# State-space scan of a hybrid decoder step: RMSNorm gains as a column table on ScalarE, sums made in y, two planes of decays instead of three

## The chip, the cores and the metric

The kernel runs on 1 core of a Trainium2 chip. The metric is the device time of one launch in microseconds (us), the median of several runs. A profiled execution of the same program gives a span (first to last instruction) and, slightly longer, a time of its own.

## The reference, cut to what matters

One layer of a decoder: a Mamba-2 branch (chunked scan), a latent attention branch, a gated merge, and a mixture of experts. Only the end of the scan branch is touched by the change. For each group `g` of 4 and each tile of tokens it computes

```
a_cs  = cumsum(dt * a)                                   # per head, within a chunk of 128 tokens
decay = exp(where(causal, a_cs[l] - a_cs[s], -inf))      # one 128x128 plane per head
y     = ((cm @ bm.T) * decay * dt) @ x  +  (cm @ h_prev) * exp(a_cs)
y     = y + ssd_d * x
y     = y * silu(z)
y     = y * rsqrt(mean(y * y, -1) + RMS_EPS) * ssd_norm_g   # RMSNorm over the 512 channels of a group
y_a   = y @ w_branch_a                                   # needs y turned: channels on partitions
```

There are 512 prompt tokens (4 tiles of 128 rows) and 64 sample tokens (8 sequences of 8, one tile of 64 rows, which start from stored states), 4 groups of 8 heads with 64 channels each.

## The kernel before

The program is a row of stages with a barrier between them: latents, two attentions, a first merge, the convolution, the scan (`stage_ssd`), a second merge, the choice of experts, the experts. Each stage is written once for each engine, and the order in an engine's code is the order of execution; engines meet only at semaphores.

The scan stage runs over 20 units. Unit `k` is group `g = k // 5` and tile `i = k % 5`; tile 4 is the sample tile. What follows uses these names.

**Decays.** `dec` holds planes of 8 heads x 128 x 128. SP (the queue of DMA requests) fills plane `k % 3` with a broadcast of rows of the running sums (`decays`, L1422 to L1426, 512 KB). VectorE subtracts each row's own sum in place (L1837, eight TENSOR_SCALAR), ScalarE takes the exponent in place (`decay`, L1683), VectorE multiplies by C.B (`weigh`, L1814), TensorE reads the plane (`outputs`, L1570). A plane is free when `y_ready` counts its unit.

**SP.** At the start it requests planes 0, 1 and 2, the gate weights of group 1, the 2 MB of stored states of group 0 and the gains of groups 0 and 1. Then for each `k` it waits for `y_ready` k + 1 and requests plane k + 3. After the sample tile of a group (`i == 4`) it goes through `new_states` (L1428 to L1434): it waits until VectorE has renewed the states, requests 2 MB of stores, waits until these stores have landed, and requests 2 MB of stored states of the next group (`old_states`, L1420). At the first tile of a group it also requests 2 MB of gate weights (L1415), waits for `normed` and requests gains (L1437).

**TensorE** in round `k`: `inputs(k)` (x, B and C.B, L1527 to L1534), `gate(k-1)` (z, L1558, the longest part), `turn(k-2)` (y turned into bank 0, L1638; waits for `normed`), `outputs(k-1)` (L1570 to L1576; gives `y_ready`, and `st_ready`).

**VectorE** in round `k`: copies and the subtraction of unit `k` (L1825 to L1837), then y of unit `k-1`: `off` = bank 5 times exp(a_cs) (L1857), y = off + xd (L1863), y += bank 4 (L1865), y *= silu(z) (L1868), the state (L1872, L1874), `weigh(k)` (L1814), and the norm: y times 1/rms times the gains `gn`, 128 x 512, broadcast to all partitions by DMA (L1889).

**ScalarE** in round `k`: `copy_x(k)` (L1678), `gate_out(k-1)` (L1696), `turned_y(k-2)` (L1702: one copy of 128x512 from bank 0 to `yT`), `decay(k)` (L1683), `root(k-1)` (L1724, L1726). Around a sample tile it also copies turned states (L1709, L1717).

**GpSimd** scales x by dt, by the end weights and by D (L1483).

Of the kernel before, what the change touches and what calls it, by code (L numbers as in the profile page):

```python
# [12 lines left out]
ALU = mybir.AluOpType  # L13
ACT = mybir.ActivationFunctionType
AX = mybir.AxisListType.X

P = 128
# [5 lines left out]
NT = 5  # L23
# [9 lines left out]
G, HG, PD, NST = 4, 8, 64, 128  # L33
SH = G * HG
GW = HG * PD
# [1317 lines left out]
def stage_ssd(nc, io, sb):  # L1353

    with ExitStack() as ctx:
        sem = ctx.enter_context(signals(nc, "ssd"))
        buf = lambda n, s: ctx.enter_context(nc.sbuf_tensor(n, s, F32))
# [3 lines left out]
        wz = (sb.wz0, buf("wz1", [P, KD, GW]))  # L1361
        m_raw, _ = merge_room(sb)
        dt_b, a_b, d_b = buf("dt_b", [P, SH]), buf("a_b", [P, SH]), buf("d_b", [P, SH])
        gn = buf("gn", [P, 2, GW])
        t1, t23 = buf("t1", [P, NT, SH]), buf("t23", [P, 2 * NT * SH])
        t2, t3 = (t23[:, NT * SH * j:NT * SH * (j + 1)].rearrange("p (i h) -> p i h", i=NT) for j in range(2))
        dta, acs, aend, e_acs, w_end, e_end = (buf(n, [P, NT, SH]) for n in ("dta", "acs", "aend", "e_acs", "w_end", "e_end"))
# [2 lines left out]
        xs_t = buf("xs_t", [P, 2, GW])  # L1370
        b_t = buf("b_t", [P, 2, NST])
        cb = buf("cb", [P, P])
        dec = buf("dec", [P, 3, HG, P])
        xdt, xend, xd = buf("xdt", [P, 2, GW]), buf("xend", [P, 2, GW]), buf("xd", [P, 2, GW])
        y = buf("y", [P, 2, GW])
        off = buf("off", [P, GW])
        zs = buf("zs", [P, GW])
        junk = zs
        ssq = buf("ssq6", [P, 2])
# [6 lines left out]
        banks = ctx.enter_context(nc.psum_tensor("banks6", [P, 8, 512], F32))  # L1386
        N = G * NT
# [5 lines left out]
        xs_ready, xs_out, cb_ready, cb_out, seg_out, dec_out, w_out = (sem(n) for n in (  # L1393
            "xs_ready", "xs_out", "cb_ready", "cb_out", "seg_out", "dec_out", "w_out"))
        scaled, of_seq, z_ready, z_out, y_ready, y_step, gated, squared, rooted, inverse, normed = (sem(n) for n in (
            "x_scaled", "of_seq", "z_ready", "z_out", "y_ready", "y_step", "gated", "squared6", "rooted6", "inverse", "normed6"))
# [2 lines left out]
            "hT_ready", "hT_out", "hT_out2", "off_part", "fin_ready", "fin_out", "hs_ready", "hs_out"))  # L1399
        e_out, y_sum, mean_ready = sem("e_out"), sem("y_sum"), sem("mean_ready")  # L1400
        rows_out, rows_in, aged = sem("rows_out"), sem("rows_in"), sem("aged")
        gn_in = [sem("gn_in0"), sem("gn_in1")]
        dec_in = [sem(f"dec_in{j}") for j in range(3)]
        heads = lambda t, n: t.rearrange("p (h d) -> p h d", h=HG)
        z_view = io.w_in.rearrange("(k p) n -> p k n", p=P)
        tri = lambda i, n: K[0:n, K_TRI:K_TRI + n] if i < 4 else K[0:n, K_BTRI:K_BTRI + n]
# [1 line left out]
        with nc.Block() as block:  # L1408
            @block.sync
            def _(sp):  # L1410
                for t, src in ((dt_b, io.dt_bias), (a_b, io.a_log), (d_b, io.d_skip)):
                    sp.dma_start(t[:], src.broadcast_to((P, SH))).then_inc(vec_in, 16)

                def z_weights(g):
                    sp.dma_start(wz[g % 2][:], z_view[:, :, C_Z + g * GW:C_Z + (g + 1) * GW]).then_inc(wz_in[g % 2], 16)  # L1415

                def old_states(g):
                    for q in range(4):
                        at = g * GW + q * P
                        sp.dma_start(h0[:, q], io.ssm[:, at:at + P, :].rearrange("b p n -> p b n")).then_inc(h_in, 16)  # L1420

                def decays(k):  # L1422
                    g, i = unit(k)
                    n = ROWS[i]
                    at = i * SH + g * HG
                    sp.dma_start(dec[0:n, k % 3, :, 0:n], io.acs_rows[at:at + HG, 0:n].unsqueeze(0).broadcast_to((n, HG, n))).then_inc(dec_in[k % 3], 16)  # L1426

                def new_states(g):  # L1428
                    sp.wait_ge(fin_out, g + 1)
                    sp.dma_start(io.o_ssmp[g * GW:(g + 1) * GW, :].rearrange("(q p) n -> p q n", p=P), st_out).then_inc(p_out, 16)  # L1430
                    sp.wait_ge(hs_out, 8 * (g + 1))
                    for q in range(4):
                        at = g * GW + q * P
                        sp.dma_start(io.o_ssms[:, at:at + P, :].rearrange("b p n -> p b n"), h0[:, q]).then_inc(h_out, 16)  # L1434

                def norm_gains(g):
                    sp.dma_start(gn[:, g % 2], io.gn[:, g * GW:(g + 1) * GW].broadcast_to((P, GW))).then_inc(gn_in[g % 2], 16)  # L1437

                z_weights(0)
                sp.wait_ge(rows_out, 1)  # L1440
                sp.dma_start(io.acs_rows[0:4 * SH, :], acsT[:, 0, :]).then_inc(rows_in, 16)
                sp.dma_start(io.acs_rows[4 * SH:5 * SH, 0:NS], acsT[0:SH, 1, 0:NS]).then_inc(rows_in, 16)
                sp.wait_ge(rows_in, 32)
                for k in range(3):
                    decays(k)
                z_weights(1)
                old_states(0)
                for g in range(2):
                    norm_gains(g)
                for k in range(N):  # L1450
                    g, i = unit(k)
                    sp.wait_ge(y_ready, k + 1)
                    if k + 3 < N:
                        decays(k + 3)
                    if i == NT - 1:
                        new_states(g)
                        if g + 1 < G:
                            sp.wait_ge(h_out, 64 * (g + 1))
                            old_states(g + 1)
                    if i == 0 and 1 <= g < G - 1:  # L1460
                        sp.wait_ge(z_ready, NT * g)
                        z_weights(g + 1)
                        sp.wait_ge(normed, NT * g)
                        norm_gains(g + 1)
                    if i == 0 and g == G - 1:
                        sp.wait_ge(z_ready, NT * g)
                        for u in range(2):
                            sp.dma_start(m_raw[:, u], merge_view(io, u)).then_inc(sb.raw_in[u], 16)
# [34 lines left out]
            def _(pe):  # L1503
# [57 lines left out]
                def outputs(k):  # L1561
# [5 lines left out]
                    if k >= 1:  # L1567
                        pe.wait_ge(y_step, 2 * k)
                    for h in range(HG):
                        pe.matmul(banks[0:n, 4, h * PD:(h + 1) * PD], dec[0:n, k % 3, h, 0:n], xdt[0:n, k % 2, h * PD:(h + 1) * PD], start=True, stop=True)  # L1570
                    if i < NT - 1:
                        pe.wait_ge(st_new, NT * g + i + 1)
                        if g >= 1 and i == 0:
# [84 lines left out]
            def _(act):  # L1658
# [21 lines left out]
                def decay(k):  # L1680
                    n = ROWS[unit(k)[1]]
                    act.wait_ge(seg_out, k + 1)
                    act.activation(dec[0:n, k % 3, :, 0:n], dec[0:n, k % 3, :, 0:n], ACT.Exp).then_inc(dec_out, 1)  # L1683

                def gate_out(j):
                    i = unit(j)[1]
# [11 lines left out]
                def turned_y(j):  # L1698
                    g, i = unit(j)
                    n = ROWS[i]  # L1700
                    act.wait_ge(yt_ready, j + 1)
                    act.activation(sb.yT[:, 4 * g:4 * g + 4, P * i:P * i + n], banks[:, 0, 0:4 * n].rearrange("p (q n) -> p q n", q=4),  # L1702
                                   ACT.Copy).then_inc(yt_out, 1)

                def last_state(g):
                    act.wait_ge(fin_ready, g + 1)
# [48 lines left out]
            def _(dve):  # L1755
# [52 lines left out]

                def weigh(k):
                    n = ROWS[unit(k)[1]]  # L1810
                    seg = dec[0:n, k % 3, :, 0:n]
                    dve.wait_ge(dec_out, k + 1)
                    dve.wait_ge(cb_out, k + 1)
                    dve.tensor_tensor(seg, seg, cb[0:n, 0:n].unsqueeze(1).broadcast_to((n, HG, n)), ALU.mult).then_inc(w_out, 1)  # L1814

                for k in range(N + 1):
                    if k < N:
# [12 lines left out]
                            dve.sem_inc(cb_out, 1)  # L1830
                        else:
                            ins.then_inc(cb_out, 1)
                        seg = dec[0:n, k % 3, :, 0:n]
                        dve.wait_ge(dec_in[k % 3], 16 * (k // 3 + 1))
                        for h in range(HG):
                            own = acs[0:n, i, g * HG + h:g * HG + h + 1]
                            ins = dve.tensor_scalar(seg[:, h, :], seg[:, h, :], own, 0.0, ALU.subtract, ALU.min)  # L1837
# [3 lines left out]
                    if k >= 1:  # L1841
# [4 lines left out]
                        if i == NT - 1:  # L1846
                            for m in range(4):
# [6 lines left out]
                                if m == 1 and k < N:  # L1854
                                    weigh(k)
                        dve.wait_ge(y_ready, j + 1)
                        dve.tensor_tensor(heads(off[0:n], n), heads(banks[0:n, 5, :], n), e_acs[0:n, i, hs].unsqueeze(2).broadcast_to((n, HG, PD)),  # L1857
                                          ALU.mult).then_inc(y_step, 1)
                        dve.wait_ge(y_step, 2 * j + 1)
                        if j >= 2:  # L1860
                            dve.wait_ge(yt_ready, j - 1)
                        dve.wait_ge(scaled, j + 1)
                        dve.tensor_tensor(y[0:n, j % 2, :], off[0:n], xd[0:n, j % 2, :], ALU.add).then_inc(y_sum, 1)  # L1863
                        dve.wait_ge(y_sum, j + 1)
                        dve.tensor_tensor(y[0:n, j % 2, :], y[0:n, j % 2, :], banks[0:n, 4, :], ALU.add).then_inc(y_step, 1)  # L1865
                        dve.wait_ge(y_step, 2 * j + 2)
# [16 lines left out]
                        if i < NT - 1:  # L1883
# [1 line left out]
                        dve.wait_ge(rooted, j + 1)  # L1885
                        dve.reciprocal(ssq[0:n, 1:2], ssq[0:n, 1:2]).then_inc(inverse, 1)
                        dve.wait_ge(inverse, j + 1)
                        dve.wait_ge(gn_in[g % 2], 16 * (g // 2 + 1))
                        dve.scalar_tensor_tensor(out=y[0:n, j % 2, :], in0=y[0:n, j % 2, :], scalar=ssq[0:n, 1:2],  # L1889
                                                 in1=gn[0:n, g % 2], op0=ALU.mult, op1=ALU.mult).then_inc(normed, 1)  # L1890
                        if i == NT - 1:
                            renew(j, 2)
                            renew(j, 3)
# [1028 lines left out]
```

## Time and profile before

| | us |
|---|---|
| median of 3 runs | 2441.16 |
| the runs | 2435.20 to 2441.32 |
| profiled execution, its own time | 2435.43 |
| its span | 2433.7 |
| mean granted TensorE clock in it | 0.965 |

The stage of the scan lies at about 669 to 975 us of the span; its units run from about 690 to 970. All times in rows are counted from the start of the span. A duration of matmuls on TensorE can overlap the next by a little. SPq rows are requests: the duration is how long SP was busy giving the request out, and the time to landing is told apart, in an answer for that line.

### The profile page before, as it was taken

How to read it: one execution, taken by the hardware profiler on the slowest of the kernel's cores; microseconds unless marked ns; L12 is line 12 of the kernel's file. 1: busy time of each engine (PE TensorE's matmuls, PEld its weight loads, DVE VectorE, ACT ScalarE, POOL GpSimd, SP SyncE). 2: the span in 40 equal slices, each digit the busy share in tenths (PEclk: the TensorE clock that was granted, in tenths of full speed). 3: DMA queues.
4: the chain of work that ended last, by engine and by line, in shares of the span. 5: the costliest groups of instructions: out<-in, count | busy, mean ns of one | idle time of the engine just before them, and what ended most of it. 6: DMA issues, size and time to landing. Idle time of an engine off the chain costs nothing. (4 is left out here: it accounts for less than half of the span.)

```text
span 2433.7 us, 38463 instructions
## 1 busy us (share of the span) xinstructions
PE 2295.1 (94%) x14433; PEld 1856.1 (76%) x14433; DVE 1841.7 (76%) x2278; ACT 1323.0 (54%) x1416; POOL 476.2 (20%) x414
## 2 busy tenths in 40 slices
PE   8898999989879998998979999999999999999997
PEld 4486778989845554997767888888888888888885
DVE  2577774167657777344578999999999999999997
ACT  1352224133245555422337777777777777777774
POOL 0003320000024443000143222122122212211223
PEclk9998998989989998998979999999999999999999
DMA  5106753232153332323559999999999999999995
GB/s 173 67 1 232 284 188 87 53 94 86 41 160 120 108 123 80 106 82 141 183 161 361 394 394 396 391 382 382 396 384 379 384 392 383 381 395 382 380 381 191
DMA packets 248676, 589.96 MB, mean 242 GB/s; under 512 B 28945, under 2 KB 120338, under 8 KB 244082
## 3 DMA queue, kind: packets, MB, share of 16 engines
q1 hardware_dynamic: 230874, 510.39, 57.3%
q0 software_dynamic: 17680, 77.88, 10.1%
q8 instruction: 84, 1.38, 0.2%
q14 instruction: 38, 0.31, 0.0%
HBM read 552.43 MB, written 35.80 MB: 242 GB/s over the span
## 5 line engine op out<-in xcount | busy, mean ns | idle before, releaser
L2694 DVE TENSOR_TENSOR w_lo<-w_raw,w_hi 128x2048 fp32r<-128x2048 f32 x291 | 658.6, 2288 | 52.7 <-ACT w_hi L2639 50.5
L2639 ACT ACTIVATE w_hi<-w_raw 128x2048 fp32r<-128x2048 f32 x288 | 550.2, 1916 | 116.5 <-PE banks L2549 89.6
L2549 PE MATMUL banks<-w_hi,x_hi 128*128 128x512 f32 x1024 | 319.5, 393 | 3.9 <-DVEq L2739 3.3
L2549 PE MATMUL banks<-w_lo,x_hi 128*128 128x512 f32 x1024 | 316.5, 390 | 0.0
L2549 PE MATMUL banks<-w_hi,x_lo 128*128 128x512 f32 x1024 | 315.9, 390 | 0.0
L2694 DVE TENSOR_TENSOR w_lo<-mergedT,w_hi 128x2048 fp32r<-128x2048 f32 x96 | 220.1, 2292 | 31.7 <-ACT w_hi L2639 31.1
L2549 PEld LDWEIGHTS banks<-w_hi,x_lo 128*128 128x128 f32 x1024 | 192.5, 188 | 40.9
L2549 PEld LDWEIGHTS banks<-w_lo,x_hi 128*128 128x128 f32 x1024 | 192.5, 188 | 40.8
L2549 PEld LDWEIGHTS banks<-w_hi,x_hi 128*128 128x128 f32 x1024 | 190.1, 188 | 42.3 <-DVEq L2739 3.7
L2497 POOL DMA_INDIRECT y_sum<-xT,to_row x31 | 51.0, 1645 | 823.5 <-ACT xT L2676 780.7
L2639 ACT ACTIVATE w_hi<-mergedT 128x2048 fp32r<-128x2048 f32 x96 | 183.8, 1915 | 33.7 <-PE banks L2549 30.7
L2549 PE MATMUL banks<-w_hi,h_hi 128*128 128x512 f32 x512 | 161.7, 397 | 1.2 <-DVE h_lo L2698 0.8
L2549 PE MATMUL banks<-w_lo,h_hi 128*128 128x512 f32 x512 | 158.8, 392 | 0.0
L2549 PE MATMUL banks<-w_hi,h_lo 128*128 128x512 f32 x512 | 158.2, 390 | 0.0
L1558 PE MATMUL banks<-wz,xT 128*128 128x512 f32 x256 | 113.6, 596 | 0.0
L2549 PEld LDWEIGHTS banks<-w_hi,h_lo 128*128 128x128 f32 x512 | 96.4, 188 | 20.9
L2549 PEld LDWEIGHTS banks<-w_lo,h_hi 128*128 128x128 f32 x512 | 96.4, 188 | 20.7
L2549 PEld LDWEIGHTS banks<-w_hi,h_hi 128*128 128x128 f32 x512 | 93.9, 189 | 19.7 <-issue 1.2
L1153 DVE TENSOR_TENSOR w_mlo_a<-wz,w_mhi_a 128x1024 fp32r<-128x1024 f32 x24 | 29.4, 1226 | 82.4 <-ACT w_mhi_a L1127 82.4
L1117 PE MATMUL banks_a<-part_hi_a,w_mhi_a 128*128 128x288 f32 x384 | 83.4, 299 | 8.8 <-DVE w_mlo_a L1153 8.8
L1558 PEld LDWEIGHTS banks<-wz,xT 128*128 128x128 f32 x256 | 47.6, 191 | 56.1 <-issue 56.1
L1483 POOL TENSOR_TENSOR xdt<-xs_t,dt 128x512 f32<-128x512 f32 (+1 forms) x20 | 27.2, 1360 | 318.7 <-ACT xs_t L1678 297.7
(511 smaller groups left out, 4591.2 us busy)
## 6 DMA issues: line engine op xcount, KB each, us to landing
w_raw<-in_exp_w_gu SPq DMA_DIRECT2D x196, 1024.0 KB, 10.3
w_raw<-in_exp_w_down SPq DMA_DIRECT2D x96, 1024.0 KB, 7.8
mergedT<-in_exp_w_gu SPq DMA_DIRECT2D x64, 1024.0 KB, 10.2
mergedT<-in_exp_w_down SPq DMA_DIRECT2D x32, 1024.0 KB, 10.0
w_x<-in_w_in SPq DMA_DIRECT2D x11, 1024.0 KB, 5.2
wz<-in_w_in SPq DMA_DIRECT2D x4, 2048.0 KB, 11.2
dec<-acs_rows SPq DMA_DIRECT2D x16, 512.0 KB, 4.2
states<-in_state_ssm SPq DMA_DIRECT2D x16, 512.0 KB, 6.8
```

Of the source, the lines that this page charges most:

```text
L1117: mm = pe.matmul(bank_of(u)[:, piece], wp[:, u % NW, k, :], part[:, piece * H2:(piece + 1) * H2], start=(k == 0 and wp is w_hi and n == 0) ...
L1153: dve.tensor_tensor(w_lo[:, u % NW], w_raw[:, u % NR], w_hi[:, u % NW].bitcast(F32), ALU.subtract).then_inc(w_low, 1)
L1483: ins = pool.tensor_tensor(heads(o[0:n, k % 2], n), x, f[:, g * HG:(g + 1) * HG].unsqueeze(2).broadcast_to((n, HG, PD)), ALU.mult)
L1558: mm = pe.matmul(banks[0:n, 7, :], sb.xT[:, q, P * i:P * i + n], wz[g % 2][:, q, :], start=(q == 0), stop=(q == KD - 1))
L2497: pool.indirect_dma_start(out=io.y_sum, out_offset=bass.IndirectOffsetOnAxis(ap=to_row[:, par, :].bitcast(U32), axis=0), in_=y_out, in_off ...
L2549: mm = pe.matmul(banks[:, bank + c, :], x[:, k, :], part[:, s % NHI, j, c * 512:(c + 1) * 512], start=start, stop=last)
L2639: act.activation(w_hi[:, s % NHI], raw(s, par), ACT.Copy).then_inc(hi_ready, 1)
L2694: dve.tensor_tensor(w_lo[:, s % NHI], raw(s, par), w_hi[:, s % NHI].bitcast(F32), ALU.subtract).then_inc(lo_ready, 1)
```

## The change

Four things, all in `stage_ssd`:

- The gains are read once as `gnT`, 128 x 16: column `t` holds the gains of channels 128t to 128t + 127. VectorE's last step is a TENSOR_SCALAR by 1/rms alone, and `turned_y` on ScalarE makes four copies of 128 columns with a column of `gnT` as scale, where it made one of 512. The first of them waits for `gnT`.
- `off` is gone: the product is written to `y`, with the wait for `yt_ready` moved ahead of it, and xd is added in place.
- `dec` has two planes, `k % 2`; SP requests 0 and 1 at the start, and plane k + 2 after `y_ready` k + 1.
- SP's waits for `normed` and its requests of gains (four of 256 KB) are gone; one request of 2048 elements of 4 bytes takes their place.

```diff
-        gn = buf("gn", [P, 2, GW])
+        gnT = buf("gnT", [P, G * 4])
-        dec = buf("dec", [P, 3, HG, P])
+        dec = buf("dec", [P, 2, HG, P])
-        off = buf("off", [P, GW])
...
-                for k in range(3):
+                for k in range(2):
                     decays(k)
                 z_weights(1)
                 old_states(0)
-                for g in range(2):
-                    norm_gains(g)
+                sp.dma_start(gnT[:], io.gn.rearrange("o (t p) -> p (o t)", p=P), allow_slow_non_contiguous=True).then_inc(gn_in, 16)
                 for k in range(N):
                     g, i = unit(k)
                     sp.wait_ge(y_ready, k + 1)
-                    if k + 3 < N:
-                        decays(k + 3)
+                    if k + 2 < N:
+                        decays(k + 2)
...
                     if i == 0 and 1 <= g < G - 1:
                         sp.wait_ge(z_ready, NT * g)
                         z_weights(g + 1)
-                        sp.wait_ge(normed, NT * g)
-                        norm_gains(g + 1)
...
                     act.wait_ge(yt_ready, j + 1)
-                    act.activation(sb.yT[:, 4 * g:4 * g + 4, P * i:P * i + n], banks[:, 0, 0:4 * n].rearrange("p (q n) -> p q n", q=4),
-                                   ACT.Copy).then_inc(yt_out, 1)
+                    if j == 0:
+                        act.wait_ge(gn_in, 16)
+                    for q in range(4):
+                        t = 4 * g + q
+                        ins = act.activation(sb.yT[:, t, P * i:P * i + n], banks[:, 0, q * n:(q + 1) * n], ACT.Copy, scale=gnT[:, t:t + 1])
+                    ins.then_inc(yt_out, 1)
...
-                        dve.tensor_tensor(heads(off[0:n], n), heads(banks[0:n, 5, :], n), e_acs[0:n, i, hs].unsqueeze(2).broadcast_to((n, HG, PD)),
+                        if j >= 2:
+                            dve.wait_ge(yt_ready, j - 1)
+                        dve.tensor_tensor(heads(y[0:n, j % 2, :], n), heads(banks[0:n, 5, :], n), e_acs[0:n, i, hs].unsqueeze(2).broadcast_to((n, HG, PD)),
                                           ALU.mult).then_inc(y_step, 1)
                         dve.wait_ge(y_step, 2 * j + 1)
-                        if j >= 2:
-                            dve.wait_ge(yt_ready, j - 1)
                         dve.wait_ge(scaled, j + 1)
-                        dve.tensor_tensor(y[0:n, j % 2, :], off[0:n], xd[0:n, j % 2, :], ALU.add).then_inc(y_sum, 1)
+                        dve.tensor_tensor(y[0:n, j % 2, :], y[0:n, j % 2, :], xd[0:n, j % 2, :], ALU.add).then_inc(y_sum, 1)
...
-                        dve.wait_ge(gn_in[g % 2], 16 * (g // 2 + 1))
-                        dve.scalar_tensor_tensor(out=y[0:n, j % 2, :], in0=y[0:n, j % 2, :], scalar=ssq[0:n, 1:2],
-                                                 in1=gn[0:n, g % 2], op0=ALU.mult, op1=ALU.mult).then_inc(normed, 1)
+                        dve.tensor_scalar(y[0:n, j % 2, :], y[0:n, j % 2, :], ssq[0:n, 1:2], None, ALU.mult).then_inc(normed, 1)
```

The order of SP's requests before, from the end of group 0's sample tile (unit 4). `states` are the stored states (`out<-states` their stores), `wz` the gate weights, `dec` a plane of decays: the one behind the states is that of unit 8, and the small one that of sample unit 9.

```order
L1430 DMA out<-states 128x4x128
L1434 DMA out<-states 128x8x128 x4
L1420 DMA states<-in_state_ssm 128x8x128 x4
L1426 DMA dec<-acs_rows 128x1024
L1415 DMA wz<-in_w_in 128x8x512
L1437 DMA gn<-in_ssd_norm_g 128x512
L1426 DMA dec<-acs_rows 64x8x64
```

The same place now:

```order
L1429 DMA out<-states 128x4x128
L1433 DMA out<-states 128x8x128 x4
L1419 DMA states<-in_state_ssm 128x8x128 x4
L1425 DMA dec<-acs_rows 128x1024
L1414 DMA wz<-in_w_in 128x8x512
L1425 DMA dec<-acs_rows 128x1024
L1425 DMA dec<-acs_rows 64x8x64
```

The request behind the states stands in the same place but is now for unit 7; the plane of unit 8 is requested behind the gate weights, where the gains were.

ScalarE before, in the round that turns the y of sample unit 4 (`xbcT` is where `yT` lies):

```order
L1678 ACTIVATE xs_t<-banks 128x512
L1696 ACT_TABLE_LOAD
L1696 ACTIVATE zs<-banks 128x512
L1702 ACTIVATE xbcT<-banks 128x4x64
L1683 ACT_TABLE_LOAD
L1683 ACTIVATE dec<-dec 128x1024
```

And now:

```order
L1671 ACTIVATE xs_t<-banks 128x512
L1689 ACT_TABLE_LOAD
L1689 ACTIVATE zs<-banks 128x512
L1699 ACTIVATE xbcT<-banks,gnT 128x64 x4
L1676 ACT_TABLE_LOAD
L1676 ACTIVATE dec<-dec 128x1024
```

One copy became four, in the same place: ahead of the exponent of the next unit's decays.

## Rows read from the trace of the kernel before

**Rows 1.** Windows: busy us (instructions) of PE, PEld, DVE, ACT, POOL; clock; DMA.

```profile
690.00:955.00 265.00, 254.67 (x1266) 146.87 (x1264) 205.78 (x428) 153.46 (x215) 103.57 (x95) 0.99 0.41 123
```

**Rows 2.** Timeline of TensorE, turns of y: start, duration, operation, [idle before, releaser].

```profile
710.67 0.66 PE L1638 MATMUL banks<-const,y 128*128 128x128 f32 x4 [1.71 <-DVE y L1889]
...
790.45 0.60 PE L1638 MATMUL banks<-const,y 128*128 128x128 f32 x4
...
858.59 0.60 PE L1638 MATMUL banks<-const,y 128*128 128x128 f32 x4
...
926.73 0.60 PE L1638 MATMUL banks<-const,y 128*128 128x128 f32 x4
```

**Rows 3.** Waits, 680 to 965 us: who waited for whom, us in total, times, longest.

```profile
PE banks L1638 <- DVE y L1889: 6.4, 5, 1.7
```

**Rows 4.** Timeline of SP's queue: start, time to give out the requests.

```profile
769.00 3.96 SPq L1434 DMA_DIRECT2D out<-states  x4
777.81 3.87 SPq L1420 DMA_DIRECT2D states<-in_state_ssm  x4
781.73 1.98 SPq L1426 DMA_DIRECT2D dec<-acs_rows  x1
...
785.12 1.85 SPq L1437 DMA_DIRECT2D gn<-in_ssd_norm_g  x1
...
849.73 1.87 SPq L1426 DMA_DIRECT2D dec<-acs_rows  x1
...
918.28 1.82 SPq L1426 DMA_DIRECT2D dec<-acs_rows  x1
```

**Rows 5.** Landings of dec (min/median/max): all; then requests at 781.73, 849.73, 918.28.

```profile
DMA to landing us min/median/max: 3.1/4.3/11.2
...
DMA to landing us min/median/max: 8.3/8.3/8.3
...
DMA to landing us min/median/max: 6.8/6.8/6.8
...
DMA to landing us min/median/max: 6.9/6.9/6.9
```

**Rows 6.** Timeline of VectorE: subtraction of unit 7, y of unit 6; a quiet subtraction.

```profile
778.22 3.65 DVE L1837 TENSOR_SCALAR dec<-dec,acs 128x128 f32<-128x128 f32 x8
782.15 0.69 DVE L1857 TENSOR_TENSOR off<-banks,e_acs 128x512 f32<-128x512 f32 x1 [0.28 <-PE banks L1575]
...
787.65 0.75 DVE L1889 SCALAR_TENSOR_TENSOR y<-y,ssq,gn 128x512 f32<-128x512 f32 x1
...
812.54 1.65 DVE L1837 TENSOR_SCALAR dec<-dec,acs 128x128 f32<-128x128 f32 x8
```

**Rows 7.** Windows, as rows 1, after stretches in which TensorE sat idle.

```profile
950.00:954.00 4.00, 4.00 (x24) 3.93 (x23) 0.69 (x1) 1.42 (x3) 1.09 (x2) 0.57 0.00 0
...
964.00:968.00 4.00, 2.19 (x6) 1.16 (x8) 2.78 (x7) 1.61 (x4) 0.00 (x0) 0.53 0.01 2
...
978.00:984.00 6.00, 5.01 (x21) 5.01 (x22) 6.00 (x9) 5.78 (x10) 0.00 (x0) 0.50 0.55 149
984.00:986.00 2.00, 2.00 (x14) 2.00 (x14) 2.00 (x3) 0.00 (x0) 0.00 (x0) 0.83 0.11 9
```

**Rows 8.** Groups of instructions by shape: busy us, mean ns of one, idle before.

```profile
L616 DVE TENSOR_SCALAR prob<-prob,den 128x512 f32<-128x512 f32 x8 | 3.9, 486 | 0.3
...
L556 ACT ACTIVATE prob<-banks,neg 128x128 f32<-128x128 f32 x8 | 2.9, 367 | 0.3 <-DVE neg L609 0.2
```

**Rows 9.** Timeline of ScalarE behind the turned y of unit 8, at sample unit 9.

```profile
814.63 0.60 ACT L1709 ACTIVATE states<-banks 128x512 f32<-128x512 f32 x1 [0.20 <-PE banks L1581]
815.51 0.60 ACT L1717 ACTIVATE h0T<-banks 128x512 f32<-128x512 f32 x1 [0.28 <-PE banks L1598]
816.41 0.60 ACT L1717 ACTIVATE h0T<-banks 128x512 f32<-128x512 f32 x1 [0.31 <-PE banks L1598]
```

**Rows 10.** Eight requests of 512 elements of 4 bytes, first stage: ns min/median/max to give out.

```profile
L213 SPq DMA_DIRECT2D page<-in_page_table x8: 487/1668/9639, 11.7 to 31.9; - x8
```

More of the change, by code:

```diff
@@ L1401, in stage_ssd @@
         rows_out, rows_in, aged = sem("rows_out"), sem("rows_in"), sem("aged")
-        gn_in = [sem("gn_in0"), sem("gn_in1")]
-        dec_in = [sem(f"dec_in{j}") for j in range(3)]
+        gn_in = sem("gn_in")
+        dec_in = [sem(f"dec_in{j}") for j in range(2)]
         heads = lambda t, n: t.rearrange("p (h d) -> p h d", h=HG)
@@ L1425, in decays @@
                     at = i * SH + g * HG
-                    sp.dma_start(dec[0:n, k % 3, :, 0:n], io.acs_rows[at:at + HG, 0:n].unsqueeze(0).broadcast_to((n, HG, n))).then_inc(dec_in[k % 3], 16)
+                    sp.dma_start(dec[0:n, k % 2, :, 0:n], io.acs_rows[at:at + HG, 0:n].unsqueeze(0).broadcast_to((n, HG, n))).then_inc(dec_in[k % 2], 16)
                 def new_states(g):
@@ L1434, in new_states @@
                         sp.dma_start(io.o_ssms[:, at:at + P, :].rearrange("b p n -> p b n"), h0[:, q]).then_inc(h_out, 16)
-                def norm_gains(g):
-                    sp.dma_start(gn[:, g % 2], io.gn[:, g * GW:(g + 1) * GW].broadcast_to((P, GW))).then_inc(gn_in[g % 2], 16)
                 z_weights(0)
@@ L1569, in outputs @@
                     for h in range(HG):
-                        pe.matmul(banks[0:n, 4, h * PD:(h + 1) * PD], dec[0:n, k % 3, h, 0:n], xdt[0:n, k % 2, h * PD:(h + 1) * PD], start=True, stop=True)
+                        pe.matmul(banks[0:n, 4, h * PD:(h + 1) * PD], dec[0:n, k % 2, h, 0:n], xdt[0:n, k % 2, h * PD:(h + 1) * PD], start=True, stop=True)
                     if i < NT - 1:
@@ L1682, in decay @@
                     act.wait_ge(seg_out, k + 1)
-                    act.activation(dec[0:n, k % 3, :, 0:n], dec[0:n, k % 3, :, 0:n], ACT.Exp).then_inc(dec_out, 1)
+                    act.activation(dec[0:n, k % 2, :, 0:n], dec[0:n, k % 2, :, 0:n], ACT.Exp).then_inc(dec_out, 1)
                 def gate_out(j):
@@ L1810, in weigh @@
                     n = ROWS[unit(k)[1]]
-                    seg = dec[0:n, k % 3, :, 0:n]
+                    seg = dec[0:n, k % 2, :, 0:n]
                     dve.wait_ge(dec_out, k + 1)
@@ L1832, in _ @@
                             ins.then_inc(cb_out, 1)
-                        seg = dec[0:n, k % 3, :, 0:n]
-                        dve.wait_ge(dec_in[k % 3], 16 * (k // 3 + 1))
+                        seg = dec[0:n, k % 2, :, 0:n]
+                        dve.wait_ge(dec_in[k % 2], 16 * (k // 2 + 1))
                         for h in range(HG):
```

## The prediction

> **What bounds the kernel now.** I read the windows first. While the units run, 690 to 955 us, TensorE is busy 254.67 of 265 us at a clock of 0.99; VectorE has 205.78 and ScalarE 153.46 [rows 1]. So the stage ends when TensorE does, and an edit on another engine counts only where TensorE waits for it. The stages around it stand behind barriers, so what the scan stage gains or loses goes through to the end. Next, TensorE's timeline: the place where it meets VectorE is the turn of y, which needs the normed y. In all it waits there 6.4 us, in 5 of the 20 rounds [rows 3]: 1.71 at unit 0 [rows 2], and 4.7 in four others, the rounds of the sample tiles, where its gate part is short. In the other rounds the turn starts with no wait: at 790.45, 858.59 and 926.73 for the second tile of groups 1, 2 and 3 [rows 2]. Third, SP's queue, which is where a plane of decays can come late.
>
> **Part 1: two planes of decays.** In a quiet round this costs nothing. A plane is requested when the unit two earlier gives `y_ready`. VectorE starts y at that moment and needs 5.50 us to its norm (782.15 to 787.65) and 0.75 for it before the next subtraction can start [rows 6], so the plane has over 6.2 us, and the median landing is 4.3 [rows 5].
>
> Behind a sample tile it is another matter. SP gives out the stores of the states at 769.00, waits until they have landed, gives out 2 MB of stored states at 777.81 and only then, at 781.73, the next plane [rows 4]. The unit whose `y_ready` allows it was done long before; SP simply stood in `new_states`. Before the change three planes cover this: that of unit 7 had been requested at unit 4, its subtraction ran at 778.22 [rows 6], and the request at 781.73 was for unit 8. Now the request at 781.73 is that of unit 7. What is ahead of it in the queue is the same, so I take its landing from the same row: 8.3 us, at 790.05, 11.8 us later than its subtraction started. VectorE stands at this wait, and behind it in its code is y of unit 6, its gating, its norm. ScalarE's exponent waits for the subtraction too, and GpSimd for y of unit 6.
>
> TensorE waits for the norm of unit 6. From the landing: 1.65 us of subtraction (the quiet one, since GpSimd has nothing to do there) [rows 6], 0.07 of gap, 5.50 to the norm, and 0.49 for it in its new form (part 2): 7.7 us. In group 1: 790.05 + 7.7 = 797.75 against a turn at 790.45, a stall of 7.3. Group 2: 849.73 + 6.8 + 7.7 = 864.2 against 858.59, 5.65. Group 3: 918.28 + 6.9 + 7.7 = 932.9 against 926.73, 6.15 [rows 2 to 5]. Sum **+19.1 us**. Group 0 has no such place. The bounds come from the landings: with the shortest, 3.1 [rows 5], each stall is about 2.1 and the sum +6.4; with 8.3 in all three groups it is +22. I take the rows of the very requests, since the queue ahead of them is unchanged. The next plane (unit 8) is now requested behind 2 MB of gate weights, where gains were requested at 785.12 [rows 4]; with the longest landing of all, 11.2 [rows 5], it is there at 796.3, and VectorE asks for it behind the norm, at about 798. It adds nothing here, and at worst about 1 in group 2.
>
> A stall of this length also costs clock. In 964 to 968, where TensorE had work for only 2.19 of 4 us, the granted clock is 0.53, that is mostly the 1.2 GHz level. Behind the barrier after the stage its work starts at about 979 (5.01 us of 978 to 984), runs at 0.50 up to 984 and at 0.83 in the next two us, so 5.7 us at the low level. In 950 to 954, behind the last group's wait, it is 0.57: 3.4 us low [rows 7]. TensorE is the bound right behind the stall (gate, outputs, inputs), so half of the low stretch is lost: 1.7 to 2.85 us, middle 2.25, three times: **+6.75 us**, bounds 0 (no fall) and +8.5.
>
> **Part 2: the norm on VectorE.** SCALAR_TENSOR_TENSOR of 0.75 [rows 6] becomes a TENSOR_SCALAR of 128x512; the same shape elsewhere takes 486 ns [rows 8]: 0.26 less per unit. It counts only at the four turns where TensorE waits for it: 4 x 0.26 = **-1.05 us**; bounds 0 and -1.4, since eight TENSOR_SCALAR that take 1.65 in a quiet place take 3.65 at 778.22, where GpSimd works too [rows 6]. The sums in y change no duration, and the moved wait (`yt_ready` of j - 1) is long fulfilled, because TensorE turns unit j - 1 before the outputs of unit j: 0.
>
> The Trainium skill (VectorE: DVE Perf Modes, the perf-mode tier table) gives fp32 TENSOR_SCALAR in SBUF twice the rate of an instruction with two tensors, 1227 against 2293 ns for 2048 elements. Scaled to 512 that would be some 430 ns, an estimate, and the term -1.3 instead of -1.05; the row goes ahead.
>
> **Part 3: the gains as a table.** Before, the norm of unit 0 waited for the first broadcast of gains, which lay behind 4 MB of weights and states; TensorE's share of that is the 1.71 us at 710.67 [rows 2]. VectorE waits no more: **-1.7 us**. What is late next is ScalarE's first `turned_y`, for `gnT`, and the plane of unit 2, now requested behind it. Giving out 4 times 512 elements takes 1.9 us by the least and 6.7 us by the median of the page-table rows [rows 10], where one broadcast of gains took 1.85 [rows 4]. The first gains landed at about 709.9, one norm (0.75) before the turn at 710.67. A third plane and a second broadcast less are in the way, and up to some 3 us of small elements more, so I put the table at 709 to 713 and the plane of unit 2 about 1 us behind it. TensorE asks for the copied y some 4 us behind the turn (now at 708.96), at about 713, and for the norm of unit 1 only a whole round later, at about 720. So the gain holds or is lost in part: -1.7 to 0 taken as bounds, and a slow table, at twice the upper end, would cost about 5 (below).
>
> The Trainium skill (DMA: Bandwidth & Descriptors, rules for kernel authors) says that a strided last dimension is lowered to one descriptor per element and should be avoided; here that is 2048 descriptors. By that rule this edit speaks against the change, but the rule has no price, and the bytes it replaces are 1 MB.
>
> **Part 4: four copies for one on ScalarE.** A copy of 128 columns from PSUM with an operand per partition is nearest to the exponent of 128x128 with such an operand, 367 ns [rows 8]; one copy of 512 columns from PSUM takes 0.60 [rows 9]. Four take 1.5 us if each starts when the last has ended, and less if they overlap, say 1.2: +0.6 to +0.9 per unit. ScalarE is busy for 58% of the stage [rows 1], and in prompt rounds the exponent and the copy of x behind it have that room. At the sample rounds the copies of turned states follow; TensorE and VectorE wait for that chain, and its own waits there are 0.20, 0.28 and 0.31, together 0.79 [rows 9]. So 0.6 is covered: 0; bounds 0 and +0.1 in each of four groups. At the end of the stage SP still gives out the last stores, 3.96 us [rows 4], longer than ScalarE's copies: 0.
>
> **Sum:** 19.1 + 6.75 - 1.05 - 1.7 = **+23.1 us**. Against the profiled execution that is 2435.4 + 23.1 = 2458.5; two of the three runs shown are nearly 6 us above it, and against the median it is 2441.2 + 23.1 = 2464.3. I give 2463.
>
> **The rivals.** (B) The same stalls, but the clock stays: +16.4, so 2452 to 2458. For it: TensorE works densely up to the stall and the 1.71 us did nothing. Against it: the fall in 950 to 954 came behind waits of TensorE shorter than any of these stalls [rows 3, 7]. 0.13. (C) More than one plane or the table is late: the plane of unit 8 or 13 lands behind the gate weights after VectorE asks for it (1 to 3 us a group), or `gnT` takes twice its upper bound (+5): +30 to +34, so 2465 to 2475. For it: the plane requested behind the gate weights took the longest of all, 11.2 [rows 5]. 0.12. (D) The other side, not slower: the late plane lands as fast as the fastest one. Place: the request at 781.73; it decides at the landing, which costs nothing up to 790.45 - 7.7 = 782.75, 1.0 us after the request. At 3.1 us each stall is 2.1, too short to bring the clock down, and the sum 6.4 - 2.75 = +3.7, 2439 to 2445. Against it: 2 MB of states stand ahead, and three rows of the same place show 6.8 to 8.3. 0.06. (E) The waits in SP's code fall otherwise than I read them, so that unit 7's plane goes out before the stores, and only the gains remain: -2.75. The order of SP's requests speaks against it. 0.02.
>
> **How the numbers follow.** Main case 0.67, B 0.13, C 0.12, D 0.06, E 0.02. A measurement of this kernel can tell about 0.3%, 7.3 us, from no change. Main, B and C are above it: slower 0.92. D and most of E are within: same 0.07; faster 0.01. The range takes in B against the lower runs less a little for landings a us shorter, and C: 2447 to 2475.
>
> **What would show it.** In the profile after: SP's request of a plane behind the states at the same distance from the stores; VectorE waiting about 12, 10 and 11 us for the DMA of `dec` in units 7, 12 and 17; TensorE waiting 5 to 8 us for the norm in the three turns behind, and a clock near 0.5 for 3 to 6 us there; no wait at the turn of unit 0; the 4.7 us at the sample rounds down to 3.6; stages outside the scan of unchanged length. Wrong would be: waits for `dec` in quiet rounds (then 4.3 us of landing is not the price), or ScalarE's copies as the releaser of TensorE.

## The result: 1.2% slower, and the profile after

| | before | after |
|---|---|---|
| median, us | 2438.18 (4 runs) | 2468.27 (4 runs) |
| the runs, us | 2432.16 to 2441.32 | 2459.54 to 2470.72 |
| span of the profiled execution | 2433.7 | 2466.5 |
| mean granted TensorE clock | 0.965 | 0.959 |

The ratio is 1.012, 95% interval 1.0086 to 1.0154: 30 us more, where 23 were forecast. The fourth run of before, 2432.16, puts its median 3 us under that of the three shown ahead of the prediction. Line numbers from here on are those of the kernel that the row is from; in the changed kernel the subtraction is L1834, the norm L1885, the turn of y L1631, ScalarE's copies of it L1699.

In this execution everything up to the scan stage came 2.2 us later than in the execution of before, so compare distances between rows, not times. SP's queue in the changed kernel (start, time to give out, request), at the place of rows 4:

```profile
771.72 3.93 SPq L1433 DMA_DIRECT2D out<-states  x4
780.54 3.90 SPq L1419 DMA_DIRECT2D states<-in_state_ssm  x4
784.48 2.03 SPq L1425 DMA_DIRECT2D dec<-acs_rows  x1
786.56 0.43 SPq L1414 DMA_DIRECT2D wz<-in_w_in  x1
787.03 50.91 SPq L1425 DMA_DIRECT2D dec<-acs_rows  x4
```

The request of a plane stands 12.8 us behind the first store, as before (12.7), and is now for unit 7. The last row holds four requests in one; its first, at 787.03, is for unit 8, and it landed 12.1 us later, at 799.1. The landing of unit 7's plane, and that of the same request in group 2 (min, median and max are of one request each; group 3 has 6.8 as well):

```profile
DMA to landing us min/median/max: 8.1/8.1/8.1
...
DMA to landing us min/median/max: 6.8/6.8/6.8
```

VectorE in the changed kernel (start, duration, operation, idle before it and what ended it), units 7, 12 and 17, with y and the norm of unit 6:

```profile
792.58 1.66 DVE L1834 TENSOR_SCALAR dec<-dec,acs 128x128 f32<-128x128 f32 x8 [11.82 <-DMA dec<-acs_rows]
794.16 0.68 DVE L1856 TENSOR_TENSOR y<-banks,e_acs 128x512 f32<-128x512 f32 x1
...
799.64 0.49 DVE L1885 TENSOR_SCALAR y<-y,ssq 128x512 f32<-128x512 f32 x1
...
870.93 1.66 DVE L1834 TENSOR_SCALAR dec<-dec,acs 128x128 f32<-128x128 f32 x8 [10.58 <-DMA dec<-acs_rows]
...
950.56 1.66 DVE L1834 TENSOR_SCALAR dec<-dec,acs 128x128 f32<-128x128 f32 x8 [10.94 <-DMA dec<-acs_rows]
```

And TensorE at the turns of y, which answer to rows 2 (units 0, 6, 7, 11 and 16):

```profile
710.81 0.60 PE L1631 MATMUL banks<-const,y 128*128 128x128 f32 x4
...
800.19 1.12 PE L1631 MATMUL banks<-const,y 128*128 128x128 f32 x4 [6.85 <-DVE y L1885]
...
816.89 0.60 PE L1631 MATMUL banks<-const,y 128*128 128x128 f32 x4
...
878.53 1.12 PE L1631 MATMUL banks<-const,y 128*128 128x128 f32 x4 [5.61 <-DVE y L1885]
...
958.16 1.12 PE L1631 MATMUL banks<-const,y 128*128 128x128 f32 x4 [5.97 <-DVE y L1885]
```

VectorE stands 11.8, 10.6 and 10.9 us for a plane, and TensorE 6.85, 5.61 and 5.97 us for the norm behind it. The turn of unit 6 takes 1.12 us where it took 0.60, and the next turn comes 16.70 us later; before the change that distance was 12.37. Windows of the changed kernel around the first stall (busy us and instructions of PE, PEld, DVE, ACT, POOL; granted clock; DMA share; GB/s) say why:

```profile
780.00:793.00 13.00, 13.00 (x52) 7.15 (x50) 1.18 (x6) 4.19 (x7) 3.18 (x3) 1.00 0.94 283
793.00:797.00 4.00, 0.33 (x1) 0.00 (x0) 3.90 (x12) 1.06 (x1) 0.00 (x0) 1.00 1.02 385
797.00:801.00 4.00, 0.81 (x4) 0.81 (x5) 3.93 (x10) 3.90 (x6) 1.15 (x2) 0.72 0.04 15
801.00:805.00 4.00, 4.00 (x19) 3.85 (x18) 3.10 (x8) 3.85 (x8) 2.03 (x3) 0.50 0.00 0
805.00:809.00 4.00, 4.00 (x9) 1.56 (x7) 2.43 (x4) 0.18 (x1) 0.00 (x0) 0.50 0.14 33
809.00:813.00 4.00, 4.00 (x26) 2.17 (x26) 3.80 (x10) 3.59 (x6) 0.84 (x1) 1.00 0.00 0
```

The clock falls while TensorE waits, and its work from 800.19 to 809 runs at 0.50, the level of 1.2 GHz: 8.8 us. Half of that is 4.4, and the round is 4.3 longer.

**Where the 33.5 us are.** The cleanest measure in a trace is the distance from the turn of unit 0 to that of unit 19: 258.86 us before, 292.33 after. By pieces, each a difference of distances between turns: the three stalls 7.0 + 5.8 + 6.1 = 18.9; the three rounds behind them (16.70, 16.73, 16.23 against 12.37) 12.55; the three sample rounds (26.0, 23.5, 24.35 against 23.09 each) 4.5; the shorter norm -0.27 in each of four rounds, -1.1; a last round that came at full clock here and not before, -1.4. Ahead of the turn of unit 0 lies the wait of 1.71 us that is gone.

### The profile page after: what moved, and what is told of

Read it like the earlier page. It is cut to its first block and busy times, and to the rows that moved or that the text cites. A ratio compares the mean times of both kernels' runs of the same rounds, so it can differ in the third digit from the quotient of the medians.

```text
span 2466.5 us, 38518 instructions
## 1 busy us (share of the span) xinstructions
PE 2308.0 (94%) x14433; PEld 1862.5 (76%) x14433; DVE 1833.7 (74%) x2278; ACT 1332.3 (54%) x1476; POOL 473.0 (19%) x414
## 5 line engine op out<-in xcount | busy, mean ns | idle before, releaser
L1476 POOL TENSOR_TENSOR xdt<-xs_t,dt 128x512 f32<-128x512 f32 (+1 forms) x20 | 23.5, 1176 | 349.5 <-ACT xs_t L1671 323.9
## 6 DMA issues: line engine op xcount, KB each, us to landing
wz<-in_w_in SPq DMA_DIRECT2D x4, 2048.0 KB, 10.9
```

Source lines behind the costliest of these rows:

```text
L1476: ins = pool.tensor_tensor(heads(o[0:n, k % 2], n), x, f[:, g * HG:(g + 1) * HG].unsqueeze(2).broadcast_to((n, HG, PD)), ALU.mult)
```

## The experiments

They ran on two other chips, A and B, on which the kernel before takes 2490 and 2491 us. Each ratio is against the kernel before on the same chip, so kernels of different chips are compared here by their ratios. The distance from the turn of unit 0 to that of unit 19 ("turns") is read from each trace. No trace of the kernel before was kept on A or B; the rounds that nothing disturbs have the same length in all traces (11.64 and 12.37, for instance, within 0.01 us).

| kernel | chip | ratio to before, 95% | turns, us |
|---|---|---|---|
| before | first | | 258.86 |
| changed, once more | B | 1.0087, 1.0055 to 1.0118 | 289.25 |
| before, two planes alone | A | 1.0101, 1.0083 to 1.0119 | |
| the same, once more | B | 1.0089, 1.0059 to 1.0119 | 287.84 |
| changed, three planes | A | 0.9993, 0.9982 to 1.0004 | 260.15 |
| changed, plane before the stores | A | 1.0058, 1.0040 to 1.0077 | 277.69 |
| changed, stall filled | A | 1.0077, 1.0053 to 1.0101 | 279.13 |
| changed, requests in another order | B | 0.9979, 0.9964 to 0.9994 | 263.95 |
| changed, three planes, copies last | B | 0.9969, 0.9955 to 0.9983 | 256.33 |

### One part alone: two planes in the kernel before

```diff
-        dec = buf("dec", [P, 3, HG, P])
+        dec = buf("dec", [P, 2, HG, P])
...
-                    if k + 3 < N:
-                        decays(k + 3)
+                    if k + 2 < N:
+                        decays(k + 2)
```

`k % 3` becomes `k % 2` wherever a plane is filled or read, and the start requests two planes.

> The kernel before with two planes of decays in place of three, and nothing else. If the late third plane carries the loss: VectorE waits 10 to 12 us for dec in units 7, 12 and 17, TensorE 5.5 to 7.5 us at the turn behind, and the clock falls there for some 8 us: 18.5 + 12.5 = +31 us over before. If the loss came from the four copies on ScalarE or from the table of gains, this kernel shows under +10 us.

> The kernel before with two planes and nothing else, once more, for its trace (the first profiled execution was disturbed): +26 to +31 us over before, waits for dec of 10 to 12 us in units 7, 12 and 17, and long rounds of 16 to 17 us behind the stalls, as in the changed kernel.

Measured: 1.0101 and 1.0089, that is +25 and +22 us by the ratios (intervals +21 to +30 and +15 to +30), where +31 and +26 to +31 were expected; in the second's trace the turns span 287.84, 29.0 more than before. Who waited for whom in that trace, 750 to 1060 us (total, times, longest):

```profile
DVE dec L1837 <- DMA dec<-acs_rows: 32.2, 4, 11.6
PE banks L1638 <- DVE y L1889: 24.3, 8, 7.2
```

The distances are those of the changed kernel: 18.92, 17.52 and 17.49 at the stalls, and 15.60, 16.21 and 16.51 behind them. Its sample rounds are 23.09 each, as before. The waits, stalls and long rounds are the expected ones (one round, 15.60, is just under 16), and the ratio is that of the changed kernel within the noise (1.0101 and 1.0089 against 1.0087): the two planes alone make the loss. The medians put it under what was expected, the turns within it.

### One part undone: three planes in the changed kernel

> The changed kernel with three planes put back. Late-plane theory: the stalls and the low clock go, +31 of the +33 us; what is left against before is -2.1 (gains no longer waited for) - 1.1 (shorter norm) + 4.5 (sample rounds, see the next call) = +1 us, 0 to +4. The theory that the rest of the change is the cost: still +20 us or more.

The edit is that of the last one, reversed. Measured: 0.9993 (0.9982 to 1.0004), and the turns span 260.15, +1.3. The ratio is -1.7 us (-4.5 to +1.0), where +1 (0 to +4) was expected; +20 or more is ruled out. In its trace, 680 to 995 us, which ends ahead of the turn of unit 18:

```profile
DVE dec L1834 <- DMA dec<-acs_rows: 4.5, 3, 2.6
...
PE banks L1631 <- DVE y L1885: 2.1, 3, 0.7
```

No stall is left; the prompt rounds in which the stalls and the low clock were are back at 11.58 and 12.37. All three sample rounds take 24.36 instead of 23.09, together +3.8. The shorter norm gives back 1.1 and a last round at full clock 1.4, which leaves the +1.3; the wait of unit 0 that is gone lies ahead of these distances.

### The plane asked for before the stores

```diff
                 def new_states(g):
...
+                    if g + 1 < G:
+                        sp.wait_ge(y_ready, NT * (g + 1) + 1)
+                        decays(NT * (g + 1) + 2)
                     sp.wait_ge(hs_out, 8 * (g + 1))
...
-                    if k + 2 < N:
+                    if k + 2 < N and (i > 0 or g == 0):
```

> The changed kernel, two planes, with SP asking for the plane of the second next tile (units 7, 12, 17) before it gives out the stores of the states instead of behind the stores' landing and the next states. If the place in SP's code is the cause and not the number of planes as such: no wait for dec in these units, no stall, as fast as the one with three planes (+0 to +4 us over before). If two planes are too few in themselves (landing against the 6 us between y_ready and the subtraction): waits for dec stay, and +10 us or more.

Measured: 1.0058, or +14 us, turns 277.69. The wait in units 7, 12 and 17 went, as expected; that the kernel would then be as fast as with three planes missed, since the expectation looked at one plane only. SP in this kernel:

```profile
823.37 0.32 SPq L1425 DMA_DIRECT2D dec<-acs_rows  x1
823.73 5.78 SPq L1436 DMA_DIRECT2D out<-states  x4
833.47 5.56 SPq L1419 DMA_DIRECT2D states<-in_state_ssm  x4
839.13 1.67 SPq L1414 DMA_DIRECT2D wz<-in_w_in  x1
840.85 44.02 SPq L1425 DMA_DIRECT2D dec<-acs_rows  x4
```

The plane of unit 7 goes out at 823.37 and nobody waits for it. But that of unit 8, the first of the four requests in the last row, goes out at 840.85, behind 2 MB of states and 2 MB of weights, and lands 11.4 us later. VectorE and TensorE wait one round later than in the changed kernel (VectorE's row, and the turns of units 7 and 12):

```profile
852.30 1.66 DVE L1837 TENSOR_SCALAR dec<-dec,acs 128x128 f32<-128x128 f32 x8 [10.96 <-DMA dec<-acs_rows]
```

```profile
859.89 1.12 PE L1634 MATMUL banks<-const,y 128*128 128x128 f32 x4 [4.10 <-DVE y L1888]
...
935.72 0.66 PE L1634 MATMUL banks<-const,y 128*128 128x128 f32 x4 [3.50 <-DVE y L1888]
```

In the last group VectorE waits 7.5 us, and the turn of unit 18 waits 3.12. In the changed kernel the first stall had hidden this second late plane: it landed at 799.1, and VectorE was busy with the norm of unit 6 until 800.1. So two requests of each later group stand behind megabytes, not one.

### Two planes, the next request ahead of the gate weights too

To the edit above comes the next plane, ahead of the gate weights. It still stands behind the stores and the stored states.

```diff
-                    if k + 2 < N and (i > 0 or g == 0):
+                    if k + 2 < N and (i > 1 or g == 0):
...
+                    if i == 0 and g >= 1:
+                        sp.wait_ge(y_ready, k + 2)
+                        decays(k + 3)
                     if i == 0 and 1 <= g < G - 1:
                         sp.wait_ge(z_ready, NT * g)
                         z_weights(g + 1)
```

> Two planes; SP asks for the planes of units 7, 12, 17 ahead of the stores and for those of 8, 13, 18 ahead of the gate weights (in the last experiment the stall had moved there, since they were asked for behind 2 MB of states and 2 MB of weights). If the place of the requests is all: TensorE waits no more than 1 us at any turn of prompt tiles, and the kernel is within 2 us of the one with three planes (0 to +2 over before). If two planes are too few: one stall of 2 us or more stays in each group.

Measured: 0.9979 (0.9964 to 0.9994). No prompt round is longer than 12.38: no stall is left. VectorE still waits 3.0 to 3.7 us for the planes of units 8, 13 and 18, but TensorE does not wait for that. The loss thus needs both, two planes and this order of requests: a third plane takes it away, and so do other places for the two requests. By the ratio the kernel is 5.2 us under before (1.5 to 9.0), where 0 to +2 over was expected. In this one trace the sample rounds take 23.46, 26.00 and 26.01 and the turns 263.95, 5 us more than before, and yet the median is under that of before; the rest of the program varies by several us from one execution to the next (the turn of unit 0 lies at 756.7 to 763.4 us in these traces), and which of the sample rounds is long varies too. Which of the two kernels, with three planes or with two, is better in the scan is not settled by this.

### The stall filled with work

```diff
+                    if g >= 1 and i == 1:
+                        pe.wait_ge(hs_out, 8 * g)
+                        for r in range(6):
+                            pe.matmul(banks[:, 2, :], K[:, K_ID:K_ID + P], K[:, K_ID:K_ID + 512], start=True, stop=True)
                     pe.wait_ge(normed, k + 1)
```

> The changed kernel, with 6 matmuls of 128x512 on constants into bank 2 (which nobody reads then) ahead of TensorE's wait for the norm in units 6, 11 and 16; they take some 5.2 us of each wait of 5.6 to 6.9. If the loss behind the stall is the clock: it stays at 1.00, the round behind takes 12.4 us and not 16.7, and the kernel gains 12 to 13 us on the changed one. If the long round behind it comes from VectorE, GpSimd or the DMA that catch up: the round stays at 16 us and the gain is 0.

> The changed kernel itself, unaltered, beside the others on this chip: 1.2% over the kernel before, three stalls of 5.6 to 7 us at the turn of units 6, 11 and 16, each with a long round (16 to 17 us) behind it. It is the measure for the filled stall (19 us over the kernel with three planes there): if the clock is worth 12.5 us, this one is 31 to 32 us over the kernel with three planes.

TensorE in this kernel, the added matmuls (the row counts twelve instructions for the six) and the turn of unit 6, and the windows around it:

```profile
841.38 5.31 PE L1629 MATMUL banks<-const 128*128 128x512 f32 x12
848.25 0.66 PE L1635 MATMUL banks<-const,y 128*128 128x128 f32 x4 [1.56 <-DVE y L1889]
```

```profile
841.00:845.00 4.00, 4.00 (x11) 1.85 (x10) 3.90 (x11) 1.06 (x1) 0.00 (x0) 1.00 1.04 391
845.00:849.00 4.00, 2.44 (x11) 1.13 (x11) 3.93 (x10) 3.84 (x6) 1.08 (x1) 1.00 0.09 34
849.00:853.00 4.00, 4.00 (x25) 2.77 (x25) 3.97 (x10) 3.86 (x8) 2.10 (x3) 1.00 0.00 0
```

The clock stays at 1.00, in the other two groups as well, and the rounds behind the stalls take 12.44, 12.43 and 12.43 us. In the trace of the changed kernel on chip B they take 16.21, 16.03 and 15.85: 10.8 us less, where 12 to 13 were expected, while the stalls themselves stay (18.45, 18.76 and 17.29 against 18.65, 17.47 and 17.64). VectorE, GpSimd and the DMA have the same work in both, so the long round is the clock. This rests on the traces. By the ratios, 1.0077 against 1.0087, the gain is 2.5 us, and the intervals overlap: they alone would not show it. Of the gain in the turns, 10.1 us, the execution with the filled stalls lost 4.0 ahead of the turn of unit 0 and 2.1 behind that of unit 19, where nothing was changed.

The changed kernel on chip B is 0.9% over before, where 1.2% was expected; its three stalls (6.91, 5.72 and 5.90) are as expected, its long rounds (16.21, 16.03, 15.85) at or just under the lower end of what was. Against the kernel with three planes it is 23 us slower by the ratios and 29.1 by the turns, where 31 to 32 were expected.

### ScalarE's copies behind the states

The kernel is the changed one with three planes; in the sample rounds the order on ScalarE becomes:

```diff
-                        turned_y(k - 2)
                         last_state(g)
                         old_state(g, 0)
                         old_state(g, 1)
                         if k < N:
                             decay(k)
                         old_state(g, 2)
                         old_state(g, 3)
+                        turned_y(k - 2)
```

> Three planes, and in the sample rounds ScalarE's four copies of turned y behind the copies of turned states instead of ahead of them. Theory from the trace of the changed kernel: the four copies hold up the copy that frees bank 6, TensorE waits 0.3 us for it, and the multiplication of the decays then meets a start of GpSimd's ageing of states (2.12 us for 1.35), so TensorE waits 2.09 for 1.31: 0.4 to 1.5 us in each of three groups. Then the wait for ScalarE is gone and the sample rounds are 1.5 us shorter each than in the kernel with three planes: 3 to 4 us under before. Rival: the copies are not what moved them, but the earlier norm; then nothing changes against the kernel with three planes (0 to -1 against before).

What it is about, in the changed kernel: ScalarE's four copies and the copy behind them, TensorE's turns of states and its next product, and VectorE's multiplication of the decays, in the first sample round.

```profile
745.78 1.14 ACT L1699 ACTIVATE xbcT<-banks,gnT 128x128 f32<-128x128 f32 x4
746.79 0.61 ACT L1706 ACTIVATE states<-banks 128x512 f32<-128x512 f32 x1
```

```profile
747.46 1.09 PE L1591 MATMUL banks<-const,states 128*128 128x128 f32 x8 [0.30 <-ACT states L1706]
...
754.47 3.54 PE L1598 MATMUL banks<-h0T,t 128*32 128x512 f32 x8 [2.09 <-DVE h0T L1850]
```

```profile
751.59 2.12 DVE L1811 TENSOR_TENSOR dec<-dec,cb 128x1024 f32<-128x1024 f32 x1 [2.31 <-ACT dec L1676]
```

A sample round, here the second, with three planes and the copies last (ScalarE, VectorE, TensorE):

```profile
862.40 0.60 ACT L1706 ACTIVATE states<-banks 128x512 f32<-128x512 f32 x1 [0.56 <-PE banks L1574]
...
868.50 1.13 ACT L1699 ACTIVATE xbcT<-banks,gnT 128x128 f32<-128x128 f32 x4
```

```profile
867.19 1.35 DVE L1811 TENSOR_TENSOR dec<-dec,cb 128x1024 f32<-128x1024 f32 x1 [2.31 <-ACT dec L1676]
```

```profile
869.29 1.91 PE L1598 MATMUL banks<-h0T,t 128*32 128x512 f32 x8 [1.32 <-DVE h0T L1850]
```

ScalarE waits for TensorE again and not TensorE for ScalarE, the multiplication takes 1.35 in all three, and all sample rounds are back at 23.09. The turns span 256.33, 3.8 less than with the copies ahead (1.3 a round, where 1.5 was expected); the shorter norm is in both kernels, so it is not what lengthened the rounds. The kernel is faster than before: 0.9969 (0.9955 to 0.9983), or 7.7 us, where 3 to 4 were expected, and faster than the changed one. It has the lowest ratio of those tried, though its interval overlaps with that of the two planes in another order.

## Why the prediction was right, point by point

- **The late plane** (part 1): right in place and size. The three landings, forecast from the very requests of before at 8.3, 6.8 and 6.9, came at 8.1, 6.8 and 6.8; the stalls, forecast as 7.3 + 5.65 + 6.15 = 19.1, cost 7.0 + 5.8 + 6.1 = 18.9. The plane of the next unit, there at 799.1 where 796.3 was forecast, added nothing, as forecast; the experiment that took the first stall away showed that only the stall covered it.
- **The clock behind the stalls** (part 1): the mechanism is right, shown by the filled stall, and this is the term that was mis-sized: 12.55 instead of 6.75, beyond its bound of 8.5. The rule used, half of the low stretch is lost, held (8.8 us low in the first group, 4.3 lost; the other two cost 4.4 and 3.9). The length was wrong: I read it from two rows where it was 3.4 and 5.7 us. The trace of before has a longer stretch at the low level with TensorE busy all through, which I had not looked for:

```profile
200.00:210.00 10.00, 10.00 (x140) 7.92 (x148) 6.39 (x10) 0.00 (x0) 8.00 (x13) 0.51 0.96 294
```

- **The norm** (part 2): 487 ns for 486 (the other estimate, 430, was too low), and -0.27 at each of the four turns: -1.1 for -1.05.
- **The gains** (part 3): TensorE's wait at unit 0 is gone, 1.7, as forecast. The table took SP 1.63 us and landed after 6.1, at about 710.7; the plane of unit 2 was late by 4.1 us for VectorE and the turn of unit 1 did not wait, as forecast.
- **The four copies** (part 4): here the sum was wrong, 0 for 4.5. The four take 1.14 us, as forecast. The step that failed was to set 0.6 us against all the idle times of ScalarE's chain together (0.79). The copy right behind the four frees a bank that TensorE waits for, and only the first of these idle times, 0.20, stands ahead of it. So 0.3 us of TensorE's time went in each of the three sample rounds. In the first and the third, VectorE's multiplication then took 2.12 us for 1.35, which cost TensorE another 0.8; in the second it took 1.23, and that round is only 0.4 longer. In the first round the clock fell as well, and a product took 3.54 for 1.91. Copies last took all of it away.
- **The sum**: 23.1 forecast, 33.5 by the turns less 1.7 for unit 0, so 31.8 in the trace, and 30.1 by the medians. The two mis-sized terms, +5.8 and +4.5, are the difference in the trace, less the 1.4 of the last round at full clock. Rival B, no fall of the clock, fell; D and E, an early plane, too. The size is that of rival C (+30 to +34), but not by C's causes: the table of gains came in time, and TensorE did not wait for the plane of unit 8 or 13. That number asked for both of C's causes at once, though C named either. So the place and the mechanism of the loss were foreseen; that the time fell into the range with two terms too small is in part luck, since its upper end had been set for C.

## What to carry to other kernels

A buffer that looks spare in steady rounds may be there for the one place where its request has to stand behind bulk transfers and a wait for their landing: before taking it out, list for each request what the issuing queue does just ahead of it, and ask that for the next request too. Then count in a stall of TensorE both the wait and the round at half clock behind it, here 18.9 + 12.55 us. A step lengthened on an engine with much idle time is free only if nothing right behind it frees a buffer that the bounding engine waits for. And when the length of a low stretch of the clock enters a sum, look for the longest one in the whole trace, not for the nearest.

## What the runs showed of the hardware that was not expected

- After waits of 5.6 to 6.9 us TensorE's work ran at the 1.2 GHz level for a whole round, 8.8 us in the first case. With work in the wait, and 1.56, 1.86 and 0.39 us of idle left, the clock stayed at 1.00.
- The same short wait did not always do the same. The wait of 2.09 us in the first sample round was followed by a product of 3.54 us and windows at 0.67 and 0.90 (the fall came with or after the wait; no run shows why there and not elsewhere); in the third sample round a wait of 2.08 was followed by 1.91 us at 1.00:

```profile
753.00:757.00 4.00, 2.53 (x7) 0.64 (x8) 1.92 (x3) 0.01 (x1) 4.00 (x4) 0.67 0.00 0
757.00:761.00 4.00, 4.00 (x20) 1.43 (x16) 2.85 (x4) 0.00 (x0) 2.63 (x3) 0.90 0.45 126
914.00:918.00 4.00, 3.05 (x13) 0.91 (x14) 2.47 (x5) 0.00 (x0) 4.00 (x4) 1.00 0.03 8
```

- VectorE's multiplication of the decays, with two inputs in SBUF, took 1.35 us in the middle of a running row of GpSimd instructions on states. When the two started together it took 2.12 us in two sample rounds of the changed kernel and 1.23 in the other, with the starts within 0.01 us of each other each time. The second round, GpSimd and VectorE:

```profile
833.71 5.15 POOL L1492 TENSOR_TENSOR states<-states,t 128x512 f32<-128x512 f32 x4 [0.23 <-PE banks L1591]
833.71 1.23 DVE L1811 TENSOR_TENSOR dec<-dec,cb 128x1024 f32<-128x1024 f32 x1 [2.31 <-ACT dec L1676]
```

  GpSimd's four take 5.15 us there and 5.05 in the rounds with 2.12. That the two engines hold each other up was read from such rows; it was not tried by itself, and what decides between the two outcomes is open.
